# Two places in a fused five-mixer kernel where TensorE's order around an attention head is changed

## What is computed

```python
# stick-breaking attention, per head and per block of 128 queries
z = q @ k.T * scale
log_fail  = where(strict, log_sigmoid(-z), 0)
log_after = reverse_cumsum(log_fail) - log_fail
w = where(strict, exp(log_sigmoid(z) + log_after), 0)
y_sb = w @ v

# memory attention, per head
qh, kh = rmsnorm(q, g_q), rmsnorm(k, g_k)
p = softmax(qh @ kh.T * scale)
y_xa = p @ vh

# how the branches meet
merged = g0 * (y_sb @ w_sb_out) + g1 * (y_ml @ w_ml_out) + g2 * (y_xa @ w_xa_out)
x = x + merged @ w_o          # g0, g1, g2 = sigmoid of h @ w_gate
```

## Time and profile before

| what | value |
|---|---|
| time, median of 3 runs | 2012.12 us (2011.96 to 2013.44) |
| the profiled execution's own time | 2010.26 us |
| its span, first to last instruction | 2008.5 us |
| PE busy | 1982.9 us, 99% of the span |
| DVE busy | 1451.0 us, 72% |
| ACT busy | 603.3 us, 30% |
| POOL busy | 348.9 us, 17% |
| granted TensorE clock, mean | 0.998 |

### The profile page before, as it was taken

How to read it: one execution, slowest core, us unless ns; L and a number is a source line. 1 busy time by engine, 2 the same in 40 slices (tenths; PEclk the granted TensorE clock), 3 DMA queues, 4 the chain that set the end, 5 groups by cost and what they waited for, 6 DMA issues and landing times.

```text
span 2008.5 us, 31639 instructions
## 1 busy us (share of the span) xinstructions
PE 1982.9 (99%) x12854; PEld 1595.8 (79%) x12854; DVE 1451.0 (72%) x2209; ACT 603.3 (30%) x1045; POOL 348.9 (17%) x317
## 2 busy tenths in 40 slices
PE   9999999999999999999999999999999999999999
PEld 7888888887777777778888877777888888888887
DVE  6666766667876777767998887676666779859973
ACT  2000122222555545423884234574310010000000
POOL 2112111111101011011111212111122212222221
PEclk9999999999999999999999999999999999999999
DMA  5333322322212122222222433221233333333332
GB/s 183 96 93 105 90 83 91 88 91 64 94 57 64 54 68 72 65 64 84 65 74 84 123 94 88 65 63 55 73 94 95 105 94 99 101 95 94 95 100 89
DMA packets 53361, 173.38 MB, mean 86 GB/s; under 512 B 6464, under 2 KB 6720, under 8 KB 53088
## 3 DMA queue, kind: packets, MB, share of 16 engines
q1 hardware_dynamic: 48112, 161.33, 26.5%
q10 hardware_dynamic: 5104, 10.03, 1.8%
HBM read 169.17 MB, written 2.16 MB: 85 GB/s over the span
## 4 chain that ended last, share of the span: by engine, by line
PE 84%; DVE 10%; ACT 3%; issue 2%; DMA 1%; ACTq 0%; DVEq 0%; SPq 0%
PE ps_lin L1935 24%; PE ps_lin L1937 23%; PE ps_lin L1936 23%; PE ps_att L1984 6%; PE ps_aux L1984 4%; DVE arena L439 3%; ACT arena L1350 2%; DVE arena L433 2%; PE ps_att L1993 2%; DVE w_lo L433 1%; DVE arena L436 1%; ACT L1356 1%; PE ps_lin L1955 1%; DVE y_lo L433 0%; PE ps_lin L1957 0%
## 5 line engine op out<-in xcount | busy, mean ns | idle before, releaser
L1935 PE MATMUL ps_lin<-xw_hi,w_hi 128*128 128x512 f32 x1704 | 689.8, 405 | 0.8 <-DVE w_lo L433 0.5
L1937 PE MATMUL ps_lin<-xw_hi,w_lo 128*128 128x512 f32 x1704 | 665.8, 391 | 0.0
L1936 PE MATMUL ps_lin<-xw_lo,w_hi 128*128 128x512 f32 x1704 | 664.9, 390 | 0.0
L415 POOL TENSOR_SCALAR w_hi<-raw 128x1024 fp32r<-128x1024 f32 (+2 forms) x309 | 345.0, 1117 | 1641.5 <-PE ps_lin L1937 1522.2
L1350 ACT ACTIVATE arena<-arena 128x512 f32<-128x512 f32 (+7 forms) x328 | 202.1, 622 | 713.1 <-DVE arena L433 323.6
L433 DVE TENSOR_TENSOR w_lo<-raw,w_hi 128x1024 fp32r<-128x1024 f32 (+2 forms) x340 | 378.2, 1115 | 45.4 <-POOL w_hi L415 17.5
L1937 PEld LDWEIGHTS ps_lin<-xw_hi,w_lo 128*128 128x128 f32 x1704 | 320.3, 188 | 68.6
L1935 PEld LDWEIGHTS ps_lin<-xw_hi,w_hi 128*128 128x128 f32 x1704 | 320.8, 188 | 67.5 <-issue 3.5
L1936 PEld LDWEIGHTS ps_lin<-xw_lo,w_hi 128*128 128x128 f32 x1704 | 321.2, 189 | 58.5
L433 DVE TENSOR_TENSOR arena<-ps_lin,rstd 128x512 f32<-128x512 f32 (+3 forms) x220 | 147.7, 671 | 193.5 <-PE ps_lin L1937 185.2
L1935 PE MATMUL ps_lin<-y_hi,w_hi 128*128 128x512 f32 (+1 forms) x544 | 205.3, 377 | 0.0
(11 more groups left out here) (188 smaller groups left out, 1676.0 us busy)
## 6 DMA issues: line engine op xcount, KB each, us to landing
raw<-in_w_up SPq DMA_DIRECT2D x44, 512.0 KB, 3.6
raw<-in_conv_w_in SPq DMA_DIRECT2D x32, 512.0 KB, 3.6
raw<-in_fox_w_in SPq DMA_DIRECT2D x32, 512.0 KB, 3.6
raw<-in_gdn_w_in SPq DMA_DIRECT2D x32, 512.0 KB, 3.6
raw<-in_w_gate SPq DMA_DIRECT2D x24, 512.0 KB, 3.6
raw<-in_swa_w_in SPq DMA_DIRECT2D x20, 512.0 KB, 3.7
raw<-in_w_ml SPq DMA_DIRECT2D x16, 512.0 KB, 3.7
raw<-in_w_down SPq DMA_DIRECT2D x16, 512.0 KB, 3.6
```

Of the source, the lines that this page charges most:

```text
L415: pool.tensor_scalar(w_whole(n, kc * c)[0], w_raw(n, kc * c), 1.0, 0.0, mult, add).then_inc(s("w_rounded"), 1)
L1935: pe.matmul(o, wh, hi, start=first and k == 0, stop=False)
L1936: pe.matmul(o, wh, lo, start=False, stop=False)
L1937: ins = pe.matmul(o, wl, hi, start=False, stop=last and k == kc - 1)
```

## The change

Four edits at two places.

Stick-breaking attention, step j = 0 only: on ACT the rectified copy of head 1 leaves `sb_logs(1)` and comes after the exponential of head 0. On PE the transposes of head 0 come after all eight pieces of their tile, not after six.

Memory attention, head 0 only: `tile(1)` ahead of the transposes becomes `tile(2)`, as in the other heads; the stretch behind the four heads has one tile less.

```diff
+            def sb_positive(n):
+
+                act.wait_ge(s("sb_logw"), n)
+                activation(sbk["pos"], sbk["L"][n % 4], ACT.Relu).then_inc(s("sb_log"), 1)
+
             def sb_logs(n):
...
                 step(activation(t, t, ACT.Exp, scale=-1.0))
                 activation(t, t, ACT.Ln, bias=1.0)
-                act.wait_ge(s("sb_logw"), n)
-                activation(sbk["pos"], L, ACT.Relu).then_inc(s("sb_log"), 1)
+                if n != 1:
+                    sb_positive(n)
...
                 sb_logs(2 * j + 1)
                 sb_weights(2 * j)
+                if j == 0:
+                    sb_positive(1)
...
-                    sb_last_tile(2 * j, 5 if j else 6)
+                    sb_last_tile(2 * j, 5 if j else 8)
...
-                tile(2 if h else 1)
+                tile(2)
...
-            tile(4 * ND)
+            tile(4 * ND - 1)
```

## The result

The changed kernel takes 2022.11 us (median of 4 runs, 2021.73 to 2022.46) against 2012.04 for the kernel before: the ratio is 1.0054, 95% interval [1.0042, 1.0066]; by the medians it is 10.1 us slower. The direction was right, the time lies outside the range. The profiled execution after took 2021.92 us (span 2020.1), 11.66 more than the one of before.

What follows compares the result with a forecast made beforehand. PE was taken as the bound, busy 1982.9 of 2008.5 us. Stick-breaking +0.97 and memory attention +5.11 gave +6.08 us, set on the median of 2012.12 for 2018.2 us; range 2014.0 to 2019.5.

Steps and rivals of the forecast that it cites:

- 0.77 + 0.20 = +0.97: Stick-breaking: the 2.40 us wait moves to the last scores; later scans plus POOL's rounding cost +0.97 us (0.77 to 1.09).
- the later scans: Stick-breaking: DVE's scans of head 1 begin 0.77 us later, behind the rectified copy, delaying the last scores of step 1.
- the first wait: Memory attention, head 0: PE's wait ahead of the first transposes goes, -2.49 us.
- the four new ones: Memory attention: PE waits for DVE's splits, 2.19, 2.18, 0.90 and 0.73 us in heads 1, 2, 3 and behind, together +6.00.
- 2.19 + 0.80: Memory attention, head 1: PE waits 2.19 us for G3's split, plus 0.80 for POOL's rounding between norm and split.
- +5.11: Memory attention's sum: -2.49 for the wait removed, +6.00 for new waits, +1.60 for POOL.
- POOL's share: Memory attention, heads 1 and 2: POOL's rounding between norm and split adds 0.80 us each, +1.60 (0 to 2.10).
- The odd splits: Memory attention: the splits of G2, G4, G6, G8 come in time, counted as nothing, with some 0.4 us of cover.
- the sum of +6.08: Both places together: stick-breaking +0.97 and memory attention +5.11 us, with +4.28 to +6.70 as ends.
- rival (d): More than counted: odd splits miss too, or the clock gives way in the 3.3 us gap; two more us, 2020; chance 0.04.

Runs made afterwards that it cites:

- run with filled gaps: The changed kernel with three unread 128x512 products on PE in each of its three long new gaps: 2015.70 us, 1.0023 to the kernel before.
- the pieces alone: The kernel before with only the eight pieces ahead of stick-breaking's transposes, ACT's order as before: 2012.38 us, 1.0006.
- the one kernel in which no wait over 1.6 us is left: The whole change with DVE's splits and ACT's copies moved forward, and three unread products in mLSTM's 2.9 us gap: 2005.72 us, 0.9971 to the kernel before.

## Why the prediction missed

**What held.** The transposes of stick-breaking lost their wait, and it came back ahead of the last scores: 18.91 us instead of 17.99, +0.92, where the forecast had 0.77 + 0.20 = +0.97. Its two terms are 0.73 for the later scans and 3.15 - 2.96 = 0.19 for POOL. In memory attention the first wait is gone and the four new ones stand where the forecast put them. By its own measure, the moment at which PE's next matmul would have begun: head 1, 1420.94 - (1417.82 + 0.23) = 2.89, where 2.19 + 0.80 was forecast. Head 2 has the same wait. The timeline's idle time is 0.16 shorter than this measure (2.73 against 2.89), so its 0.72 and 0.57 in head 3 and behind it stand for 0.88 and 0.73, where 0.90 and 0.73 was forecast. Together with the 2.49 that went that is +4.90, against +5.11. POOL's share is 1.94 - 1.23 = 0.71 per head, forecast 0.80. The odd splits hold, as assumed: no wait for them is left. The run with filled gaps, where the waits stand alone, has 1.0023, some 4.6 us with an interval of 2.8 to 6.4: the sum of +6.08 lies in it.

The rule from the Trainium skill ("SBUF — State Buffer", "SBUF: two separate sides") that the forecast weighed, a port pair locked for a whole instruction, agrees with the rows: in head 1 POOL's record begins 0.21 us into the norm and is 1.45 long instead of 1.05, and the split behind the norm is the one that stands still. Each held the other up, one after the other. The size is near that of the trace before (0.71, against 0.80 in the earlier trace rows) and not POOL's full operation, and no run here tests the rule apart from these rows.

**What failed** is one step, the pricing of the new gaps: the sum has no term for TensorE's clock. The forecast counted a microsecond of waiting as a microsecond, and gave the rest to rival (d), "the clock gives way in the new gap of 3.3 us", with 0.04 and two more microseconds. The clock did give way, and in three gaps. Stick-breaking: 8.79 - 6.40 = 2.39 us behind the last scores. Head 1: from 1420.94 to 1424.28 are eight matmuls, 3.34 us, which at 0.23 are 1.84, so about 1.5 more. Head 2: from 1446.97 to 1454.19 are 24 matmuls, 7.22 us, which at 0.23 are 5.52, so 1.7 more. In the profiled executions the sum of the waits is then +0.92 + 4.90 = 5.82 us and that of the clock 2.39 + 1.5 + 1.7 = 5.6 us, together 11.4 of the 11.66 us. The forecast had the first at 6.08 and the second at nothing.

**Why the chance was wrong.** The argument for 0.04 was that the new gap would be longer than the longest of the trace, 2.9 us, as though that one were harmless. It was not: the row of the clock for 1180 to 1190 reads 0.66, and behind that gap the matmuls begin 0.43 us apart. The forecast read the list of waits without that view. With it, three new gaps of some 3 us would each have had a price on top of their length, and the case with the clock would have been the forecast and not a rival with 0.04. The Trainium skill ("TensorE: Matmul & The Clock Gate", "Part 1: The HAM clock gate (the "warmup" mystery)") says that the clock is set by how busy the array has been; these runs agree: with unread products in the gaps, stretches that stood at 0.66 stand at 1.00 in two kernels.

## What to carry to other kernels

Before a wait is moved, ask what the engine will meet next, and bring that chain forward in the same change: here the same PE edits cost 10 us alone and gave 4 to 5 us once four splits, four copies and the emptying of a tile had moved with them. Ask whether a PE gap costs more than its length, and read the granted clock behind gaps of its size in the trace at hand; in this kernel gaps of 2.7 to 2.8 us cost 1.5 to 2.4 us on top. If a long gap can't be closed, products that nobody reads can be a remedy, but they must be shorter than the gap: they gave 6.4 us in the changed kernel, and in the gap of 2.9 us of the kernel before a gain whose interval ends at no change.

## What the runs showed of the hardware

The clock's fall isn't a matter of the gap's length alone, and it differs between executions. In the profiles of this case the granted clock fell behind the new gaps of 2.7 and 2.8 us each time (seven of seven), behind mLSTM's 2.9 us in seven of eleven kernels that had it unfilled, and behind the 2.3 us ahead of memory attention's first transposes in three of six. Behind the old 2.25 us in stick-breaking it never fell (four kernels), but it did behind the two gaps of 0.90 and 1.59 us with 5 us of work between them, in the kernel with the pieces alone. That is also what a good part of the spread between runs of one kernel is likely to be: in 71 runs of the kernel before, those with a mean granted clock of 0.999 took 2010.3 us (median of 38), those with 0.998 2011.7 (29), and those with 0.997 from 2012.5 to 2014.9 (4); and the one kernel in which no wait over 1.6 us is left has six runs within 1.1 us.

An operation of 1.05 us on POOL can cost DVE's chain anything between 0.19 and 0.86 us, by where it falls among DVE's scans. Two edits that look independent decide that: the pieces alone let POOL go at the start of the scans, and the exchange then moves the scans away from it.
